# A two-layer trunk's RWKV-7 recurrence: triangular blocks of 16 instead of 8, with work moved from GpSimd to VectorE

## What is computed

```python
def step(S, xs):
    r_t, w_t, k_t, v_t, a_t, b_t = xs
    sa = jnp.einsum('bhvk,bhk->bhv', S, a_t)
    S = S * w_t[:, :, None, :] + sa[..., None] * b_t[:, :, None, :] + v_t[..., None] * k_t[:, :, None, :]
    return S, jnp.einsum('bhvk,bhk->bhv', S, r_t)
```

## Time and profile before

| | us |
|---|---|
| median of three runs (lowest, highest) | 2944.12 (2941.83, 2952.87) |
| profiled execution, its own time | 2945.5 |
| span of the profile, first to last instruction | 2943.8 |
| TensorE busy in it | 2691.4 |
| VectorE busy | 1306.2 |
| ScalarE busy | 558.2 |
| GpSimd busy | 485.5 |

### The profile page before, as it was taken

The page is one execution under the profiler, slowest core; times in us unless marked ns, Lnnn a source line. Parts: engine busy times, 40 slices in busy tenths (PEclk is TensorE's granted clock), DMA queues, the critical chain, the costliest instruction groups (busy, mean ns, idle before and its releaser), DMA issues. The chain is left out here.

```text
span 2943.8 us, 60987 instructions
## 1 busy us (share of the span) xinstructions
PE 2691.4 (91%) x26020; PEld 1538.1 (52%) x26020; DVE 1306.2 (44%) x2324; ACT 558.2 (19%) x1552; POOL 485.5 (16%) x654
## 2 busy tenths in 40 slices
PE   5699989999979599999889999999999999999996
PEld 1367767666657589998744444333333333333332
DVE  1667576676626466665323114422233232222333
ACT  2100011022005355555422111100000000000002
POOL 0104000000015466675131000000000000000000
PEclk8899999999989789999989999999999999999998
DMA  9567555544627312211098878899999999999999
GB/s 408 223 211 212 191 171 196 215 179 179 220 63 154 134 40 48 68 49 45 21 355 339 306 291 341 314 400 403 403 403 404 404 399 394 401 404 405 405 413 353
DMA packets 263749, 777.50 MB, mean 264 GB/s; under 512 B 99986, under 2 KB 161065, under 8 KB 195329
## 3 DMA queue, kind: packets, MB, share of 16 engines
q1 hardware_dynamic: 251216, 712.63, 64.2%
q0 software_dynamic: 11968, 61.92, 7.0%
q10 hardware_dynamic: 368, 0.10, 0.0%
HBM read 707.81 MB, written 66.77 MB: 263 GB/s over the span
## 5 line engine op out<-in xcount | busy, mean ns | idle before, releaser
L2276 PE MATMUL oe_ps<-experts_ring,tail_arena 128*32 128x512 f32 x4096 | 500.2, 603 | 43.2 <-DMA experts_ring<-in_w_up 43.1
L620 DVE SCALAR_TENSOR_TENSOR pj_macc<-pj_mring,head_cond_t,pj_macc 128x1024 f32<-128x1024 f32 x240 | 297.0, 1278 | 186.5 <-DMA pj_mring<-in_w_ada 186.5
L2276 PEld LDWEIGHTS oe_ps<-experts_ring,tail_arena 128*32 128x32 f32 x4096 | 150.7, 111 | 341.2 <-issue 340.1
L732 PE MATMUL pj_ps<-head_hT,head_ring_in 128*128 128x320 f32 x1104 | 312.1, 436 | 6.6 <-DVE head_hT L593 4.2
L2309 PE MATMUL oe_ps<-experts_ring,oe_hidt 128*32 128x512 f32 x2880 | 312.0, 592 | 0.0
L2284 PE MATMUL oe_ps<-experts_ring,tail_arena 128*32 128x512 f32 x2048 | 272.2, 598 | 0.0
L732 PEld LDWEIGHTS pj_ps<-head_hT,head_ring_in 128*128 128x128 f32 x1104 | 210.8, 191 | 96.0 <-DVE head_hT L593 6.6
L2648 DVE SCALAR_TENSOR_TENSOR oe_hid_s<-oe_hid_s,oe_gcol_s,oe_ps 128x512 f32<-128x512 f32 x16 | 12.0, 747 | 534.6 <-ACT oe_hid_s L2490 534.6
L2381 PE MATMUL oe_ps<-experts_ring,tail_arena 128*128 128x512 f32 x480 | 220.8, 609 | 17.4 <-DMA experts_ring<-in_w_out 12.9
L732 PE MATMUL pj_ps<-pj_t,pj_s 128*128 128x320 f32 x736 | 210.3, 439 | 7.0 <-DVE pj_t L599 7.0
L2309 PEld LDWEIGHTS oe_ps<-experts_ring,oe_hidt 128*32 128x32 f32 x2880 | 108.0, 110 | 201.0 <-issue 201.0
(11 more groups left out here) (414 smaller groups left out, 3952.7 us busy)
## 6 DMA issues: line engine op xcount, KB each, us to landing
experts_ring<-in_w_gate SPq DMA_DIRECT2D x128, 1024.0 KB, 23.9
experts_ring<-in_w_up SPq DMA_DIRECT2D x128, 1024.0 KB, 26.2
experts_ring<-in_w_down SPq DMA_DIRECT2D x128, 1024.0 KB, 22.6
experts_ring<-in_w_out SPq DMA_DIRECT2D x68, 1024.0 KB, 7.3
pj_mring<-in_w_ada SPq DMA_DIRECT2D x64, 1024.0 KB, 9.7
head_ring_in<-in_w_in SPq DMA_DIRECT2D x23, 2048.0 KB, 8.5
ada_ring<-in_w_ada SPq DMA_DIRECT2D x16, 2048.0 KB, 19.5
scratch_z<-pj_stage POOLq DMA_DIRECT2D x19, 640.0 KB, 8.0
```

Source lines behind the costliest of these rows:

```text
L620: a = nc.vector.scalar_tensor_tensor(acc, w, scalar, acc, ALU.mult, ALU.add)
L732: mm = pe.matmul(bank(name, b)[:, 0:TH], a[:, k, :], h[:, k, :], start=(k == 0), stop=(k == KH - 1))
L2276: pe.matmul(ps[32 * i:32 * i + 32, bank, :], xe[:, k, GROUPS[i % 2]], w[:, kk * DE + 512 * (i // 2):kk * DE + 512 * (i // 2) + 512], start ...
```

## The change

- The diagonal blocks are 16 tokens instead of 8. `blk` now has one block a partition: 2 heads x 10 chunks x 4 blocks = 80 partitions, 16x16 each. The solve has 14 steps instead of 6. The scratch in DRAM is laid out by chunks, so that a block starts every `STRIDE = 1040` elements.
- The first level (8 to 16) goes; two are left.
- The copy back into `comp` is two DMAs (one a head) of 64-byte pieces; it waits for the placing of the unit before.
- `shift`, `kd` and `place` go from GpSimd to VectorE: the shift right ahead of the scan, `kd` ahead of `removal`'s product, each half's placing ahead of its turn. `scaled_r` takes over a wait for the loads.
- The hand-written order of a round is new: the first turn comes after the fourth score eviction, the second after the fifth, the levels later.
- The constants need fewer masks.

```diff
@@ recurrence_constants: the masks of one size of block instead of two
-    for i in (3, 4):
-        n = 2 ** i
...
+    n = hb // 2
...
@@ block_rwkv
-    SB = 8
-    FIRST_LV, LAST_LV = 2, 4
+    SB = 16
+    NBK, STRIDE = 2 * NCK * CK // SB, SB * CK + SB
+    FIRST_LV, LAST_LV = 3, 4
     STEPS = 2 * (SB - 2)
-    MOVED, ZEROS = 5 * 16, NT * 16
+    MOVED, ZEROS = 6 * 16, NT * 16
@@ plan
-        items = [w0, a0, w1, a1, s0, "slot", "scan", sc[0], "slot", sc[1], "slot", sc[2], turn0, "slot", sc[3], turn1, "slot", lv["x", 0, 2], sc[4], "slot", lv["x", 1, 2], "slot", "removal",
-                 lv["d", 0, 2], bk[0], "slot", lv["d", 1, 2], "slot", "exp_in", lv["x", 0, 3], bk[1], "slot", lv["x", 1, 3], "exp_inv", "slot", "pad_b", lv["d", 0, 3], bk[2], "slot", "half0",
-                 lv["d", 1, 3], "exp_ex", "slot", "half1", "pad_k", lv["x", 0, 4], vt[0], "slot", "decay", lv["x", 1, 4], "slot", "far", lv["d", 0, 4], vt[1], "slot", "pad_a", lv["d", 1, 4], "slot", "slot"]
+        items = [w0, a0, w1, a1, s0, "slot", "scan", sc[0], "slot", sc[1], "slot", sc[2], "slot", sc[3], turn0, "slot", sc[4], turn1, "slot", "slot", "removal",
+                 lv["x", 0, 3], bk[0], "slot", lv["x", 1, 3], "slot", "exp_in", "slot", lv["d", 0, 3], bk[1], "slot", "half0", lv["d", 1, 3], "exp_inv", "slot", "half1", "pad_b", bk[2], "slot",
+                 "exp_ex", lv["x", 0, 4], "slot", "pad_k", lv["x", 1, 4], vt[0], "slot", "decay", "slot", "far", lv["d", 0, 4], vt[1], "slot", "pad_a", lv["d", 1, 4], "slot", "slot"]
@@ SP, blocks_out
-                    sp.dma_start(lb_d[h, 0:CK * NCK * CK].rearrange("(s c t) -> s c t", s=CK, t=CK), sc[HEADS[h], u % NS, :, 0, 0:CK]).then_inc(moved, 16)
+                    dst = lb_d[h].rearrange("(c y) -> c y", c=NCK)[:, 0:CK * CK].rearrange("c (s t) -> s c t", t=CK)
+                    sp.dma_start(dst, sc[HEADS[h], u % NS, :, 0, 0:CK]).then_inc(moved, 16)
...
-                src = lb_d.rearrange("h (b x) -> (h b) x", b=SB)[:, 0:SB * NCK * CK].rearrange("g (n t) -> g n t", t=CK)
-                sp.dma_start(blk[:, 0:SB * NCK * SB].rearrange("g (n k) -> g n k", k=SB), src[:, :, 0:SB]).then_inc(moved, 16)
+                src = lb_d.rearrange("h (b y) -> (h b) y", y=STRIDE)[:, 0:SB * CK].rearrange("n (i t) -> n i t", t=CK)
+                sp.dma_start(blk[:, 0:SB * SB].rearrange("n (i k) -> n i k", k=SB), src[:, :, 0:SB]).then_inc(moved, 16)
@@ SP, blocks_back
-                sp.wait_ge(tinit, MADE + (STEPS + 3) * u + STEPS + 1)
-                sp.dma_start(tb_d, blk[:, 0:SB * NCK * SB]).then_inc(moved, 16)
+                sp.wait_ge(tinit, MADE + (STEPS + 1) * u + STEPS + 1)
+                sp.dma_start(tb_d, blk[:, 0:SB * SB]).then_inc(moved, 16)
                 sp.wait_ge(moved, ZEROS + MOVED * u + 64)
-                sp.dma_start(comp[:].rearrange("p c k -> p (c k)"), tb_d.rearrange("g (i x) -> (g i) x", i=SB)).then_inc(moved, 16)
+                if u:
+                    sp.wait_ge(placed, 2 * u)
+                for h in range(2):
+                    src = tb_d[h * NBK // 2:(h + 1) * NBK // 2, :].rearrange("(c b) (i k) -> (b i) c k", c=NCK, k=SB)
+                    sp.dma_start(comp[HEADS[h]], src).then_inc(moved, 16)
@@ GpSimd: shift, kd and place are gone; scaled_r
+            def scaled_r(v):
+                pool.wait_ge(ex_done, 3 * v + 1)
                 if v % 2 == 0:
                     pool.wait_ge(loads, (v // 2 + 1) * NLOAD)
@@ GpSimd, solve: the same two instructions a step, on [NBK, ...] without the chunk axis
-                    nc.gpsimd.tensor_tensor(part, t[:, rows, :, j:j + 1].to_broadcast(shape), t[:, j:j + 1, :, cols].to_broadcast(shape), ALU.mult).then_inc(tinit, 1)
+                    nc.gpsimd.tensor_tensor(part, t[:, rows, j:j + 1].to_broadcast(shape), t[:, j:j + 1, cols].to_broadcast(shape), ALU.mult).then_inc(tinit, 1)
                     pool.wait_ge(tinit, n + 2 * s + 1)
-                    nc.gpsimd.tensor_tensor(t[:, rows, :, cols], t[:, rows, :, cols], part, ALU.add).then_inc(tinit, 1)
+                    nc.gpsimd.tensor_tensor(t[:, rows, cols], t[:, rows, cols], part, ALU.add).then_inc(tinit, 1)
@@ VectorE
+            def place(v, b):
+                dve.wait_ge(moved, ZEROS + MOVED * (v + 1))
+                if v:
+                    dve.wait_ge(dve_ev, RANK[G["d", 1, LAST_LV, v - 1]])
+                    dve.wait_ge(spread, own_spread(v - 1))
+                shape = [P, BC, HB // SB, SB]
+                nc.vector.tensor_tensor(chunks(tt, b).rearrange("p c (g k) -> p c g k", k=SB), chunks(comp, b).unsqueeze(2).to_broadcast(shape),
+                                        kept[:, 0, 0, :].rearrange("p (g k) -> p g k", k=SB).unsqueeze(1).to_broadcast(shape), ALU.mult).then_inc(placed, 1)
...
             def scan(v):
+                dve.wait_ge(act_ev, RANK[G["w", 1, v]])
+                nc.vector.tensor_scalar(sg[:], sg[:], 1.0, 1.0, ALU.add, ALU.mult).then_inc(shifted, 1)
                 dve.wait_ge(shifted, v + 1)
...
             def removal(v):
                 dve.wait_ge(act_ev, RANK[G["a", 1, v]])
                 dve.wait_ge(loads, (v // 2 + 1) * NLOAD)
+                dve.wait_ge(par_ready, 2 * (v // 2) + 2)
+                nc.vector.tensor_scalar(kd[:], ar[:], pp[:, 1:2], pp[:, 9:10], ALU.mult, ALU.add).then_inc(bk_done, 1)
+                dve.wait_ge(bk_done, 2 * v + 1)
+                nc.vector.tensor_tensor(kd[:], kd[:], kt[:], ALU.mult).then_inc(bk_done, 1)
...
                     elif item in ("turn0", "turn1"):
                         b = int(item[-1])
-                        dve.wait_ge(tinit, MADE + (STEPS + 3) * (u - 1) + STEPS + 1 + b + 1)
+                        place(u - 1, b)
+                        dve.wait_ge(placed, 2 * (u - 1) + b + 1)
                         turn(u - 1, b)
```

More of the change, by code:

```diff
@@ L270, in recurrence_constants @@
     ch.link(nc.gpsimd.memset(join[:], 1.0))
-    for i in (3, 4):
-        n = 2 ** i
[L273 to L281, removed]
+    n = hb // 2
+    for rows in groups:
+        m = join[rows, 4, :].rearrange("p (b n) -> p b n", n=n)
+        ch.link(nc.gpsimd.affine_select(out=m, in_=m, compare_op=ALU.is_ge, fill=0.0, base=0,
+                                        pattern=[[-n, hb // n], [0, n]], channel_multiplier=1))
+        ch.link(nc.gpsimd.affine_select(out=m, in_=m, compare_op=ALU.is_ge, fill=0.0, base=n - 1,
+                                        pattern=[[n, hb // n], [0, n]], channel_multiplier=-1))
+    ch.link(nc.gpsimd.tensor_scalar(kept[:, 0, 0, :], join[:, 4, :], 1.0, None, ALU.mult))
+    ch.link(nc.gpsimd.tensor_tensor(join[:, 4, :], join[:, 5, :], join[:, 4, :], ALU.subtract))
     for g, rows in enumerate(groups):
@@ L284, in recurrence_constants @@
             ch.link(nc.gpsimd.memset(half[rows, h:h + 1], 1.0 if h == g % 2 else 0.0))
-    for i in (3, 4):
-        for h in range(2):
-            ch.link(nc.gpsimd.tensor_scalar(kept[:, i, h, :], join[:, i, :], half[:, h:h + 1], None, ALU.mult))
+    for h in range(2):
+        ch.link(nc.gpsimd.tensor_scalar(kept[:, 4, h, :], join[:, 4, :], half[:, h:h + 1], None, ALU.mult))
     ch.link(nc.gpsimd.memset(kept[:, 5:7], 0.0))
@@ L1251, in block_rwkv @@
             ("wd", "we", "ud", "ue", "zd", "oe", "sr"))
-        shifted = sem("shifted")
+        shifted, placed = sem("shifted"), sem("placed")
         fo_out, osum_done, o_out = sem("foout"), sem("osum"), sem("oout")
@@ L1342, in _ @@
                 pool.sem_inc(s, 1)
-            def shift(v):
-                pool.wait_ge(act_ev, RANK[G["w", 1, v]])
-                nc.gpsimd.tensor_scalar(sg[:], sg[:], 1.0, 1.0, ALU.add, ALU.mult).then_inc(shifted, 1)
             def front(v):
@@ L1379, in solve @@
             def solve(v):
-                t = blk[:, 0:SB * NCK * SB].rearrange("g (i c k) -> g i c k", c=NCK, k=SB)
-                n = MADE + (STEPS + 3) * v
+                t = blk[:, 0:SB * SB].rearrange("n (i k) -> n i k", k=SB)
+                n = MADE + (STEPS + 1) * v
                 pool.wait_ge(moved, ZEROS + MOVED * v + 48)
@@ L1386, in solve @@
                     rows, cols = (slice(j + 1, SB), slice(0, j)) if v % 2 else (slice(0, j), slice(j + 1, SB))
[L1387 to L1388 removed]
+                    shape = [NBK, SB - 1 - j if v % 2 else j, j if v % 2 else SB - 1 - j]
+                    part = prod[:, 0:shape[1] * shape[2]].rearrange("n (i k) -> n i k", k=shape[2])
                     if s:
                         pool.wait_ge(tinit, n + 2 * s)
[L1391 removed]
+                    nc.gpsimd.tensor_tensor(part, t[:, rows, j:j + 1].to_broadcast(shape), t[:, j:j + 1, cols].to_broadcast(shape), ALU.mult).then_inc(tinit, 1)
                     pool.wait_ge(tinit, n + 2 * s + 1)
[L1393 to L1405 removed]
+                    nc.gpsimd.tensor_tensor(t[:, rows, cols], t[:, rows, cols], part, ALU.add).then_inc(tinit, 1)
+                nc.gpsimd.memset(blk[:].rearrange("n (i x) -> n i x", x=SB + 1)[:, :, 0:1], 1.0).then_inc(tinit, 1)
```

(9 more changed lines are left out.)

23 lines of the change are left out of this document (3 added, 20 removed).

## The result

The changed kernel takes 2969.38 us (median of six runs, 2963.22 to 2971.19) against 2945.26 us before (six runs): a ratio of 1.0070, 95% interval 1.0056 to 1.0085 (the ratio is estimated over the single runs; the medians alone give 1.0082). By the medians that is 24 us slower, past the 14.7 us taken as "the same" and outside the forecast range. The profiled execution took 2971.19 us, its span 2969.1.

The account below looks back on a forecast made before the run. TensorE was taken as the bound (47.5 of 50 us busy, 27.34 us a round), a slower five-queue circle behind it. Twelve rounds give -12.5 us, the ends +6.8: -6, so 2938 us, range 2916 to 2962.

Parts of the forecast that it names:

- The first link: GpSimd's queue: the solve ends 3.15 us later, and so does the `tw` half behind it.
- The circle through GpSimd's order: Score eviction, SP's transfers, solve, then GpSimd's `tw` half by program order, needed by TensorE; some 4 us of slack.
- the gap at the first `u` stage: Sign that the forecast is right: a new TensorE gap there, released by GpSimd's `tw`.
- the late `tw`: GpSimd's half comes 1.35 us late; 0.62 falls into TensorE's gap, 0.7 us a round is lost.
- SP's odd rounds: Every second round SP's ten loads behind the copy-back make the scores 0.95 us late: rounds of 25.85 and 26.8 us.
- That much stays: GpSimd's solve: the old stalls beside VectorE, about 1.1 us, carry over, so 9.5 becomes 10.6 us.
- the scan catches the solve: Rival: VectorE's scan holds what GpSimd has left; solve 12.2 us, 2960 us; chance 0.22.
- the cover of the key factors: VectorE's key factors stand behind score evictions while TensorE has other work; covered unless the next pair's loads land late.
- the placing set aside as hidden with 1.3 us spare: VectorE's placing costs nothing: copied blocks land at +8.5, 1.3 us before its first turn.
- The gain on offer: TensorE loses one level, four jobs of 0.56 us a unit: 2.2 us of 27.34, a round of 25.1.
- TensorE stays the bound: Rival: with a solve of 10 us or less, 26 us come off twelve rounds, 2921 us; chance 0.30.
- The ends: Start and end of the recurrence, where nothing covers the longer solve and copy: 3.4 us each, 6.8 both.

Follow-up runs that it names:

- e11: The changed kernel with 10 of the 14 elimination steps of each solve, the last four left out: 2935.33 us, ratio 0.9967 to before.
- e2: The changed kernel with SP's four key loads ahead of the even unit's copy-back, the other six behind the odd unit's scores: 2955.29 us, ratio 1.0027.
- e1: The changed kernel with GpSimd making its half of the previous unit's `tw` ahead of the solve instead of behind it: 2998.42 us, ratio 1.0164.
- e3: The changed kernel with the edits of e1 and e2 together: 2968.45 us, ratio 1.0071 to before.
- e5: The changed kernel with ScalarE making the half of `tw` that GpSimd made behind the solve: 2963.44 us, ratio 1.0074 to before.
- e14: e9 with six output buffers instead of four, and 10 of the 14 elimination steps of each solve: 2936.71 us, ratio 0.9959 to before.
- e15: e9 with six output buffers instead of four, and every `x` job's 20 matmuls issued twice: 2964.69 us, ratio 1.0058 to before.
- e9: e7 with GpSimd's sum of the two directions' outputs behind the next unit's front instead of right behind the solve: 2949.21 us, ratio 1.0018.
- e7: The changed kernel with the edits of e2 and e5, and the fifth score job and eviction ahead of the first placing and turn: 2948.28 us, ratio 1.0008.

## Why the prediction was wrong

**The first link held; what it cost the round did not.** The circle through GpSimd's order is there, with the gap at the first `u` stage; so are SP's late scores, the 9.5 us of the undisturbed solve, the prices on VectorE (shift 0.49, factor 0.61 and 0.83, placing 0.32) and TensorE at 43.7 of 50 us. But the prediction ended with "A round under 24.5 or over 28.5 us would make the whole account wrong", and at 28.89 it was. The step that failed leads from the solve's end to the length of the round: behind a solve of 10.6 us the prediction priced only the late `tw` (0.7 us) and SP's odd rounds (0.95 in every second), and came to 26.3. A straight line through the change (solves of 11.5 us, rounds of 28.89) and e11 (8.4, 26.44) gives an estimate of 28.2 us for a solve of 10.6. So the solve's own size was the lesser part of the miss.

**The solve: 10.6 taken, 11.5 measured.** The text took the old stalls of 1.1 us over unchanged ("That much stays"). But a solve that lasts longer stands beside more of VectorE's work. Of the 2.0 us over the undisturbed 9.44, these products make some 1.6 in the mean, and the scan, which holds one operation up to 1.15 us in four solves of twelve, some 0.4. This is near the rival "the scan catches the solve", which turned the sign at 11.1 us and gave 2960 for 12.2; it was given 0.22 and was the nearest of the four, though the scan was the smaller part.

**SP's odd rounds.** The scores were taken to leave 0.95 us late; 1.45 in the mean was measured, 3.1 at worst. The larger part was the cover of the key factors. The text said "their cover goes if the loads for the next pair land late" and priced it at nothing, though its own sum had the loads issued later. VectorE waited 1.7 us for them in the mean, TensorE up to 4.1; e2, which takes both away, gives back 14 us, 1.1 us a round.

**The circle was cut short.** It was followed from the solve to `tw`, with the placing set aside as hidden with 1.3 us spare. In the change itself the first placing waited for its blocks in only two of the twelve steady rounds (2.2 and 0.9 us). But as soon as `tw` is out of the way (e1, e3, e5), the fifth score behind the placing closes a second loop, and it takes back what was gained.

**The clock was not in the sum.** The prediction had no term for it, and its 2.2 us were read at a clock of 1.00. Waits of TensorE brought stretches at the lower level, which the estimate above puts at some 0.9 us a round.

**The gain on offer: 2.2 us taken, about 1 found.** With no named circle left all rounds but one are 25.9 to 26.6 us, not 25.1 (e14; that e15 pays for half of the doubled work fits it). From before to e14 TensorE's idle time goes from 1.4 to 2.0 us a round: part of the removed matmuls had filled time in which it would have waited for its own stages. And its busy time falls by 1.5, not 2.2 (by 1.6 in e9, at the full clock); why, stays open. Rival "TensorE stays the bound" (2921) was thus not on offer in full in any of these runs.

**The ends: 6.8 taken, 1.5 measured.** The trip is paid, as TensorE's first wait for turned blocks shows (9.3 us against 4.0). That the last units win it back because they lack their third level too, with nothing else to wait for, is an argument; no run takes it apart.

**Outside the recurrence** (the span less the stretch from the first round's start to the end of the last sum of outputs) 6.8 us came that no step has. The three profiles with the old blocks have 2452.5 to 2454.4 us there, the fourteen with the new ones 2456.0 to 2466.8. In the change 2.5 us lie ahead of the first round, where the shorter making of the constants was priced at nothing, and TensorE's later wait for `o` from DRAM is 7.6 us instead of 4.5. Its cause was not sought and stays open. Two more things no run tells: what the new order of a round costs by itself, with the old blocks, and what a solve of 16x16 blocks in fewer operations would give. e11 and e14 leave work out and only show what one of about 8 us would be worth, some 10 us below the kernel before.

## What to carry to other kernels

When an operation on a shared in-order engine gets longer, follow its end through every queue behind it, its own engine's and those it releases, until a path closes on itself; the slack of one reader is not the slack of all. Work that moves to an engine takes its waits along: a wait on a load that cost nothing on an idle engine stops everything queued on a busy one. Work taken off the bounding engine is worth only what its idle gaps do not take back. Issuing that work twice tells how much: here 0.4 to 0.5 of its time, in a run that came late, though the kernel before could have been asked first.

## What the runs showed of the hardware

**A wait of TensorE can be paid twice.** The granted clock behind the 4.1 us wait, in slices of 1 us of the changed kernel (PE busy first, clock third from the right):

```profile
1322.00:1323.00 1.00, 0.00 (x0) 0.00 (x0) 1.00 (x3) 0.00 (x0) 0.00 (x0) 1.00 0.04 7
1323.00:1324.00 1.00, 0.78 (x16) 0.78 (x16) 0.56 (x2) 0.00 (x0) 0.00 (x0) 0.63 0.49 47
1324.00:1325.00 1.00, 1.00 (x24) 1.00 (x24) 0.43 (x2) 0.00 (x0) 0.17 (x1) 0.50 0.39 35
1325.00:1326.00 1.00, 1.00 (x24) 1.00 (x22) 0.24 (x1) 0.00 (x0) 0.72 (x4) 0.50 0.00 0
1326.00:1327.00 1.00, 1.00 (x30) 1.00 (x28) 0.28 (x1) 0.59 (x1) 0.76 (x3) 0.66 0.00 0
1327.00:1328.00 1.00, 1.00 (x38) 1.00 (x37) 0.68 (x4) 0.82 (x4) 0.81 (x3) 1.00 0.00 0
```

The clock falls from 2.4 to 1.2 GHz here as the work comes back. 20 `x` matmuls, 32 transposes and 16 matmuls of the stages, up to the next `x`, took 1326.80 - 1323.22 = 3.58 us; the same row of work takes 1233.76 - 1231.78 = 1.98 at the full clock. So the wait of 4.1 us cost 1.6 more. It is no rule of one wait: behind the waits of 2.13 us (1221.04) and 2.15 us (1307.91) the clock stayed at 1.00, behind one of 1.12 us (1377.20) it fell, and in the wait of 3.78 us that ends at 1079.30 it fell before the work came back (0.50 from 1078 to 1079). Before, the clock was 1.00 in every 50 us window of the steady rounds; the change has 0.97 over 250 us.

**The hold between VectorE and GpSimd goes both ways, and takes one-input operations too.** A GpSimd sum held VectorE's shift 1.3 us (1.79 against 0.49, e7), the scan held a GpSimd addition 1.15 us, and VectorE's second key product took 2.03 us instead of 0.83 beside GpSimd's 1.78 us product (1319.57, where 1.54 is usual). The rows of the products above show the same for a chain of small operations: 9.44 us undisturbed, 10.9 us or more beside VectorE's work. The rule that the prediction cited and left out of its sum (the Trainium skill, SBUF — State Buffer, Who interferes with whom: a `tensor_scalar` in a two-port mode takes the shared pair as well) agrees with the 1.79 us. The other way the change shows less than the 0.5 us that the prediction worked out by it: beside the shift a solve operation took 0.2 us longer (0.43 instead of 0.22, 1134.96).
